# Delta rule on unnormalised queries and keys, with block-diagonal solution and score matrices in its scan

## The reference

```python
def l2_normalize(x):
    return x * lax.rsqrt(jnp.sum(x * x, axis=-1, keepdims=True) + EPS)

def gdn_direction(q, k, v, beta, g):          # 4 heads of 128, chunks of c = 64 tokens
    gc = cumsum(g per chunk)
    decay = exp(gc_i - gc_j) for i >= j, else 0
    kb = k * beta
    lower = strictly lower part of (kb @ k.T) * decay
    u, w = solve(lower + eye, [v * beta, kb * exp(gc)])
    def step(state, ...):
        v_new = u - w @ state
        scores = (q @ k.T) * decay
        out = (q * exp(gc)) @ state + scores @ v_new
        state = state * exp(g_last) + (k * exp(g_last - gc)).T @ v_new
    ...
q, k, v = split(silu(centred_depthwise_conv(q | k | v)))
q = l2_normalize(q) * HD ** -0.5 ; k = l2_normalize(k)
o = forward direction + backward direction
o = o * rsqrt(mean(o * o) + EPS) * norm_g ; y = o * silu(z)
```

## Time and profile before

| | us |
|---|---|
| median of 3 runs | 1723.66 (1723.11 to 1725.65) |
| the profiled execution | 1726.8 |
| its span, first to last instruction | 1725.0 |
| busy: PE, DVE, ACT, POOL | 1687.7, 1160.1, 950.6, 10.1 |

### The profile page before, as it was taken

The page is one execution under the profiler, slowest core; times in us unless marked ns, Lnnn a source line. Parts: engine busy times, 40 slices in busy tenths (PEclk is TensorE's granted clock), DMA queues, the critical chain, the costliest instruction groups (busy, mean ns, idle before and its releaser), DMA issues.

```text
span 1725.0 us, 24744 instructions
## 1 busy us (share of the span) xinstructions
PE 1687.7 (98%) x10220; PEld 1390.6 (81%) x10220; DVE 1160.1 (67%) x1833; ACT 950.6 (55%) x1475; POOL 10.1 (1%) x22
## 2 busy tenths in 40 slices
PE   8999999999999999999999999999999999999998
PEld 6777888877778887888888888888888888878886
DVE  6876886679688667555686467655575556885554
ACT  6743643577155446444566657544464456974443
POOL 0000000000000000000000000000000000000000
PEclk8999999999999999999999999999999999999999
DMA  6322445442234555555644234645555555445543
GB/s 237 123 100 85 178 147 199 171 174 108 77 141 147 191 189 185 193 182 184 220 175 155 100 121 173 234 176 191 218 184 194 186 200 210 148 165 190 191 177 145
DMA packets 41728, 291.77 MB, mean 169 GB/s; under 512 B 4656, under 2 KB 4912, under 8 KB 7440
## 3 DMA queue, kind: packets, MB, share of 16 engines
q1 hardware_dynamic: 39168, 280.23, 45.0%
q0 software_dynamic: 2304, 8.91, 1.5%
q10 hardware_dynamic: 144, 1.05, 0.2%
HBM read 289.12 MB, written 1.05 MB: 168 GB/s over the span
## 4 chain that ended last, share of the span: by engine, by line
PE 81%; DVE 13%; ACT 4%; issue 2%; DMA 0%; DVEq 0%; SPq 0%; ACTq 0%
PE pg L476 24%; PE pg L478 24%; PE pg L477 23%; DVE wl L1948 3%; PE ps L824 2%; PE ps L643 2%; ACT wh L1314 1%; PE ps L867 1%; PE ps L627 0%; ACT hTh L1642 0%; PE ps L926 0%; PE ps L1211 0%; PE ps L1166 0%; DVE hTl L2528 0%; DMA x<-x_in 0%
## 5 line engine op out<-in xcount | busy, mean ns | idle before, releaser
L476 PE MATMUL pg<-wh,hTh 128*128 128x512 f32 x2096 | 836.7, 399 | 5.5 <-DVE wl L2031 3.6
L478 PE MATMUL pg<-wh,hTl 128*128 128x512 f32 x2096 | 819.6, 391 | 0.0
L477 PE MATMUL pg<-wl,hTh 128*128 128x512 f32 x2096 | 818.9, 391 | 0.0
L1948 DVE TENSOR_TENSOR wl<-raw,wh 128x1024 fp32r<-128x1024 f32 x518 | 609.6, 1220 | 191.5 <-ACT wh L1314 188.6
L1314 ACT ACTIVATE wh<-raw 128x1024 fp32r<-128x1024 f32 x528 | 528.8, 1054 | 202.9 <-DMA raw<-weights 192.4
L476 PEld LDWEIGHTS pg<-wh,hTh 128*128 128x128 f32 x2096 | 394.8, 188 | 90.2 <-issue 8.3
L478 PEld LDWEIGHTS pg<-wh,hTl 128*128 128x128 f32 x2096 | 394.7, 188 | 84.5
L477 PEld LDWEIGHTS pg<-wl,hTh 128*128 128x128 f32 x2096 | 395.2, 189 | 75.5
L1414 ACT ACTIVATE arena<-pg,sm 128x256 f32<-128x256 f32 (+1 forms) x67 | 36.6, 546 | 237.7 <-PE pg L478 237.6
L2615 DVE SCALAR_TENSOR_TENSOR arena<-pg,sm,arena 128x256 f32<-128x256 f32 x88 | 38.5, 479 | 155.0 <-ACT arena L1415 155.0
L1369 ACT ACTIVATE hTh<-ps 128x512 fp32r<-128x512 f32 x60 | 33.6, 597 | 31.5 <-PE ps L643 31.5
(11 more groups left out here) (383 smaller groups left out, 1140.1 us busy)
## 6 DMA issues: line engine op xcount, KB each, us to landing
raw<-weights SPq DMA_DIRECT2D x265, 1024.0 KB, 4.8
arena<-wide POOLq DMA_DIRECT2D x9, 512.0 KB, 3.6
raw<-weights ACTq DMA_DIRECT2D x1, 1024.0 KB, 5.5
x<-x_in SPq DMA_DIRECT2D x2, 512.0 KB, 7.5
cst<-const_tables POOLq DMA_DIRECT2D x1, 1024.0 KB, 5.3
plainh<-dist_tables POOLq DMA_DIRECT2D x2, 512.0 KB, 5.7
arena<-gate_mix POOLq DMA_DIRECT2D x1, 1024.0 KB, 7.9
arena<-token_mix POOLq DMA_DIRECT2D x2, 256.0 KB, 5.0
```

The costliest lines, as they stand in the source:

```text
L476: pe.matmul(dst, lh, rh, start=first, stop=False)
L477: pe.matmul(dst, lh, rl, start=False, stop=False)
L478: return pe.matmul(dst, ll, rh, start=False, stop=last)
L1948: tt(wl[:, slot, h], raw[:, slot, h], wh[:, slot, h], ALU.subtract)\
```

## The change

Queries and keys are not normalised any more. The SiLU results of the convolution, which have channels on the partitions, are themselves `qnT` and `knT`; the turns of `features` and their copies fall away, and ScalarE copies the turned-back k into `kn`. VectorE computes all 16 norms at once (`norms`), and they are put where vectors of the right shape are: beta times the key norm (`BETA_NK`) multiplies the values `VS`, half of them on VectorE, half on GpSimd; beta times its square (`BETA_NK2`) takes the place of beta in the lower matrix and goes into `NEGS`; the query norms go into the output's own normalisation. `TB` isn't multiplied by beta any more.

In the scan each head's two 64x64 matrices stand on the diagonal of one 128x128 matrix (`T_DIAG`, `SC_DIAG`), whose other half GpSimd fills with zeros. The scores and the last additions of the inverse are written there by more and smaller instructions; ScalarE copies a part of the inverse. The core of the diff:

```diff
-                gemm(..., inside={(0, 1): second_turn, (1, 0): first_features, (1, 1): cumulated,
-                                                       (1, 3): back_and_rows})
+                gemm(..., inside={(0, 1): second_turn, (1, 1): cumulated, (1, 3): back_and_rows})
...
-                prepare(3)
-                c.wait("qk_ready")
-                features(kn, 2)
-                prepare(3)
-                c.wait("feat_read")
+                prepare(6)
+                c.wait("sq_ready")
+                c.wait("kn_ready")
                 turn_back(2)
...
+                c.wait("vs_ready")
+                c.wait("inv_copied")
+                c.wait("zeros_ready")
...
                     for h in range(NH):
-                        for d, m, r in places[t]:
-                            rhs = RV[half(r), ...] if t else VS[half(r), 0, ...]
-                            last = pe.matmul(ps[half(r), 0, ...], TB4[half(r), 4 * d + h, m, :], rhs, ...)
+                        rhs = RV[:, h * P:(h + 1) * P] if t else VS[:, 0, h * P:(h + 1) * P]
+                        last = pe.matmul(ps[:, 0, h * P:(h + 1) * P], t_diag[:, h, :], rhs, ...)
...
# ScalarE
-                features(qnT, 0)
                 convolved(1)
                 square(1)
+                for m in range(M):
+                    last = act.activation(kn[:, 512 * m:512 * m + 512], ps[:, 2 + m, :], ACT.Copy)
+                last.then_inc(sem["kn_ready"], 1)
...
+                c.wait("inv_yt", 5)
+                for m in range(M):
+                    for r in range(2):
+                        dst, _ = diagonal(2 * m + r)
+                        last = act.activation(dst[half(r), 2:4, half(r)], new[half(r), m], ACT.Copy)
+                last.then_inc(sem["inv_copied"], 1)
# VectorE
-                normalized(0, qn)
...
-                normalized(1, kn)
+                norms()
...
-                    last = dve.tensor_copy(VS[half(r), t, :], ps[half(r), 2 + m, :])
+                    last = tt(heads(VS[half(r), t, :]), heads(ps[half(r), 2 + m, :]), over(BETA_NK[half(r), o:o + 4], P), ALU.mult)
...
-                for d, js in enumerate(both):
-                    last = tt(SC3[:, js, :], SC3[:, js, :], ps[:, 1, :]..., ALU.mult)
+                for r in range(2):
+                    tt(SC6[half(r), :, r, :, half(r)], SC5[half(r), 0], QK4[half(r)], ALU.mult)
+                    for m in range(M):
+                        last = tt(SC6[half(r), 1 - m, 1 - r, :, half(r)], SC5[half(r), 1, m], QK4[half(r), m], ALU.mult)
...
-                c.step(ts(NEGS, EGS, -1.0, None, ALU.mult))
+                for t in range(1, 4):
+                    for d in range(2):
+                        last = stt(NEGS[half(r), 4 * t:4 * t + 4], EGS[half(r), 4 * t:4 * t + 4], -1.0,
+                                   BETA_NK2[half(r), o:o + 4], ALU.mult, ALU.mult)
...
+                c.step(tt(STATS, STATS, NQ2, ALU.mult))
                 rstd_of(STATS, HD)
+                c.step(tt(STATS, STATS, NQ, ALU.mult))
# GpSimd
+                pool.wait_ge(sem["rs_ready"], l + 1)
+                for t in range(4):
+                    for v in diagonal(t):
+                        for r in range(2):
+                            last = pool.memset(v[half(r), :, half(1 - r)], 0.0)
+                last.then_inc(sem["zeros_ready"], 1)
+                c.wait("norms_ready")
+                c.wait("back_read")
+                for t, d in ((0, 0), (1, 0), (2, 1), (3, 1)):
+                    v = heads(VS[half(r), t, :])
+                    last = pool.tensor_tensor(v, v, over(BETA_NK[half(r), o:o + 4], P), ALU.mult)
+                last.then_inc(sem["vs_ready"], 1)
```

More of the change, by code:

```diff
@@ L350, in small_parts, with diagonal @@
             return sw[:, 0:KD * 2 * n].rearrange("p (k t n) -> p k t n", k=KD, t=2)
+        def diagonal(t):
+            cols = 512 * (t % 2)
+            return (heads(v) for v in (T_DIAG[t // 2][:, cols:cols + 512], SC_DIAG[:, 512 * t:512 * t + 512]))
         def times(ap, n):
@@ L397, in program @@
         Lm, LT, X_, XT_, TM_ = V(5120), V(6144), V(7168), V(8192), V(9216)
[L398 removed]
+        SC_, LMASK, SC_DIAG = XT_, TM_, xn
         STATE = V(5120)
@@ L872, in gdn @@
                     for h in range(NH):
[L873 to L876 removed]
+                        rhs = RV[:, h * P:(h + 1) * P] if t else VS[:, 0, h * P:(h + 1) * P]
+                        last = pe.matmul(ps[:, 0, h * P:(h + 1) * P], t_diag[:, h, :], rhs, start=True, stop=True)
                     last.then_inc(sem["uw_done"], 1)
@@ L891, in gdn @@
                     for h in range(NH):
-                        for d, m, r in places[t]:
-                            last = pe.matmul(ps[half(r), 1, h * P:(h + 1) * P], SC4[half(r), 4 * d + h, m, :],
-                                             VN[half(r), h * P:(h + 1) * P], start=True, stop=True)
+                        last = pe.matmul(ps[:, 1, h * P:(h + 1) * P], sc_diag[:, h, :], VN[:, h * P:(h + 1) * P],
+                                         start=True, stop=True)
                     last.then_inc(sem["sv_done"], 1)
@@ L2168, in gdn @@
                     m, r = scan_chunk(t, d)
-                    last = dve.tensor_copy(VS[half(r), t, :], ps[half(r), 2 + m, :])
+                    o = 8 * m + 4 * d
+                    last = tt(heads(VS[half(r), t, :]), heads(ps[half(r), 2 + m, :]), over(BETA_NK[half(r), o:o + 4], P),
+                              ALU.mult)
                 last.then_inc(sem["v_read"], 1)
@@ L2234, in gdn @@
                         c.wait("inv_y")
-                        n = ps[:, 2:4, 256:512].rearrange("p g (q f) -> p g q f", f=CHUNK)
-                        tt(X5[:, :, 1], X5[:, :, 1], n, ALU.add)
-                        c.wait("inv_yt")
[L2238 to L2247, removed]
+                        old, new = (v.rearrange("p g (h m f) -> p m g h f", m=M, f=CHUNK)
+                                    for v in (X_.rearrange("p (g n) -> p g n", g=2)[:, :, 256:512], ps[:, 2:4, 256:512]))
+                        for m in range(M):
+                            for r in range(2):
+                                dst, _ = diagonal(3 - 2 * m - r)
+                                tt(dst[half(r), :, half(r)].rearrange("p (g h) f -> p g h f", g=2), old[half(r), m],
+                                   new[half(r), m], ALU.add)
+                        c.wait("inv_yt")
+                        old, new = (v.rearrange("p (h m f) -> p m h f", m=M, f=CHUNK)
+                                    for v in (XT_[:, 0:256], ps[:, 0, 0:256]))
+                        for m in range(M):
+                            for r in range(2):
+                                dst, _ = diagonal(2 * m + r)
+                                last = tt(dst[half(r), 0:2, half(r)], old[half(r), m], new[half(r), m], ALU.add)
+                        c.sig(last, "inv_scaled")
                 prepare(1)
```

73 lines of the change are left out of this document (36 added, 37 removed).

## The result

| kernel | median | runs | lowest to highest | profiled execution | its span |
|---|---|---|---|---|---|
| before | 1723.74 us | 6 | 1722.92 to 1725.65 | 1726.80 | 1725.0 |
| after | 1730.50 us | 6 | 1727.96 to 1732.28 | 1729.91 | 1728.1 |

The ratio is 1.0028 with a 95% interval of 1.0019 to 1.0038: slower by 3.3 to 6.6 us. The prediction said 1729.5.

The account below looks back on a forecast made before the run. VectorE was taken to bound the kernel up to the inverse, TensorE behind it. GpSimd's contention of +6.0 us and -0.2 for the rest gave +5.8, so 1729.5 us from a 1723.7 median; 80% range 1720.5 to 1734.5.

Parts of the forecast that it names:

- case (a): Whole kernel: GpSimd's multiplies hold up VectorE, +6.0 us, the rest -0.2; 1729.5 us, chance 0.47.
- Rival (b): Whole kernel: GpSimd's work is free and the other effects cancel; 1723.5 us, chance 0.33.
- Part 7: GpSimd's multiplies before the inverse hold up three VectorE instructions: 3.0 us a layer lost, 6 in all.
- Part 1: q's norm and turns go, before k's taps on VectorE: 1.85 us a layer gained of 5.2 removed.
- Part 2: k's norm becomes `norms` on VectorE: 0.7 us lost, 0.37 gained at v's turn; `low_ready` 1.55 us sooner so far.
- Part 3: Scores written into block diagonals on VectorE, between `low_ready` and the inverse: 2.7 us for 1.29, 1.4 a layer lost.
- Part 4: End of the inverse on VectorE: additions 2.4 us against 2.6, 0.1 gained; `NEGS` as six instructions, 0.4 lost.
- Part 5: Scan's products on full matrices: bursts still 1.00 us, entering cheaper by 0.13 each; five count, 0.65 a layer gained.
- rival (c): Scan's full-matrix bursts cost by instructions, under 0.7 us each: about 5.5 us faster in all, 1718.2, chance 0.15.
- Part 6: Output's norm: two more small dependent instructions before `y_ready`, 0.4 us a layer lost.
- parts 1 to 6: All effects but GpSimd's contention, from q's norm to the output's: 0.1 us a layer gained, 0.2 in all.
- Rival (d): TensorE's longer waits drop its clock to 1.2 GHz as the inverse starts: 1.7 us a layer more, 1733, chance 0.05.

Follow-up runs that it names:

- e1: The kernel after with GpSimd's four multiplies of the values left out (output not the reference's): 1725.66 us, 1.0004 of before.
- e2: The kernel after with the four multiplies made by ScalarE late in the inverse instead of by GpSimd: 1724.96 us, 0.9999 of before.
- e8: The kernel after with GpSimd's four multiplies held back until the second level of the inverse: 1725.03 us, 0.9995 of before.
- e3: The kernel before with the same four GpSimd multiplies added at the same place, by ones: 1733.22 us, 1.0041 of before.
- e5: e2 without the block diagonals and zero fills; scan, scores and end of the inverse as before: 1719.71 us, 0.9964 of before.
- e4: The kernel after without GpSimd's multiplies, its sixteen write-only zero fills moved to their place: 1725.94 us, 1.0005 of before.
- e6: e5 with VectorE's retention masks and `NEGS` moved into the levels of the inverse: 1715.38 us, 0.9946 of before.
- e7: The kernel before with only the retention masks moved into the levels of the inverse: 1721.27 us, 0.9981 of before.

## Why the prediction was right, and where its terms were not

The forecast was case (a), GpSimd in VectorE's way, with all else cancelling. The first half is shown by experiments: with the multiplies gone, done elsewhere, or done later, the change is at 1.0004, 0.9999 and 0.9995 of before (e1, e2, e8); with the multiplies alone, the kernel before loses 4.8 to 9.1 us (e3). Rival (b), GpSimd free, falls with e3 and e8. The second half, the cancelling, came out in the sum, with help from a term that the prediction didn't have.

The profiled executions can be divided at four instructions of each layer: from the start of the convolution of q to the end of `low_ready`, on to the first step's copy of the new values (L2267), on to the last step's copy, and on to TensorE's product at `y_ready` (L643). Each cell has the first and the second layer, in us:

| kernel | to `low_ready` | to the first copy | to the last copy | to L643 |
|---|---|---|---|---|
| before | 52.46, 52.64 | 48.69, 48.48 | 33.42, 33.44 | 25.27, 25.03 |
| after | 53.69, 53.86 | 49.59, 51.72 | 32.26, 32.26 | 25.43, 25.43 |
| e8 | 51.14, 51.31 | 49.57, 51.34 | 32.24, 32.25 | 25.43, 25.43 |
| e3 | 55.77, 55.94 | 49.34, 49.32 | 33.43, 33.41 | 25.26, 25.04 |
| e5 | 51.16, 51.32 | 46.38, 46.34 | 33.41, 33.41 | 25.42, 25.42 |

After takes 1.1 us more than before in the first layer and 3.7 in the second, 4.8 together, which is what the ratio says; the rest of that pair of executions differs by 1.7 the other way. The first column shows the contention alone: 2.55 us a layer between e8 and after, 3.3 between before and e3. By parts:

- **Part 7, contention.** Taken at 3.0 us a layer as three VectorE instructions held up, the second L1948 and both L2178. It was these three, each held up by 0.83 to 0.85 us and not by 1.0: 2.5 us. GpSimd's instruction was allowed 1.38; alone it takes 1.05, beside VectorE 1.7. The Trainium skill (SBUF — State Buffer, Who interferes with whom) says that a VectorE instruction with two SBUF inputs contends with a GpSimd instruction that reads SBUF and not with one that only writes. The runs agree: the pair L2175 takes 2.98 beside the multiplies and 1.29 beside the fills of e4, and L2178, with an input in PSUM, 1.23 beside the multiplies. The estimate of 3.4 us a layer by the page's figure for GpSimd came from nearly the right duration (1.1 estimated, 1.05 measured), but VectorE lost 2.5 us, less than the whole of three of them.
- **Part 1.** 1.85 us a layer predicted. In the second layer the convolution of q starts 0.87 later than before (VectorE's first taps at 363.77 against 362.90), and k's sum 0.92 sooner (388.91 against 389.83): 1.8 gained.
- **Part 2.** `norms` takes 5.81 us (from 388.91 to 394.72) against 5.01 before. The predicted loss of 0.7 had the 0.2 of beta's copy already taken off; on the same terms 0.6 were lost. The 0.37 for L709's lateness brought 0.1: VectorE's own L1944 ends at 400.72 and L2166 follows at once, so VectorE hadn't been waiting for TensorE there. `low_ready` comes 1.2 later, counted from the same start (2.10 - 0.87); less the contention's 2.5 that is 1.3 sooner, not 1.55. The new wait at the turn of v was taken at 1.7 and is 1.65.
- **Part 3.** The scores take 2.7 us, as worked out, by four rows of VectorE from 421.27 to 424.0, of which these are the first two:

```profile
421.27 0.68 DVE L2197 TENSOR_TENSOR xn<-arena,ps 64x512 f32<-64x512 f32 x1
421.88 0.73 DVE L2199 TENSOR_TENSOR xn<-arena,ps 64x256 f32<-64x256 f32 x2
```

- **Part 4** was mis-sized. The eight last additions take 2.9 us and not 2.4 (a pair of 64x256 0.85, a pair of 64x128 0.6), so 0.3 is lost where 0.1 was to be gained; TensorE waits 0.7 for them (L870). `NEGS` costs 3.25 - 2.48 = 0.77 from the start of L1944 to that of L2275, where I had 0.4: each of the six costs 0.14.
- **Part 5** was mis-sized the other way. A burst of the scan on full matrices, by TensorE's timeline of after, against the earlier trace rows:

```profile
471.84 0.39 PE L486 MATMUL pg<-wh,hTl 128*128 128x512 f32 x1
472.07 1.05 PE L886 MATMUL ps<-arena,xn 128*128 128x128 f32 x8
472.88 0.48 PE L484 MATMUL pg<-wh,hTh 128*128 128x512 f32 x1
```

  It holds TensorE for 472.88 - 472.07 = 0.81 us, not 1.00, and its entry takes 0.23 as predicted. So a burst saves 0.3 us and not 0.13. My row for it, L941 of the retention stage, had 0.2 more; it was followed by another burst on full matrices, and whether that is the reason isn't shown. This is a part of rival (c), which wanted under 0.7. The gain did arrive: from the first copy to the last the scan is 1.2 us a layer shorter, in every kernel with block diagonals, where 0.65 was predicted.
- **Part 6.** 0.4 us were to be lost at `y_ready`. From the scan's last copy to L643's product the kernel after takes 0.2 and 0.4 us more. TensorE's wait there grew from 0.2 in all to 1.9, by more than that, since TensorE is there earlier.
- **A stop of TensorE that the prediction left out.** The prediction called TensorE nearly always busy in the inverse, with short waits. The view behind the earlier trace rows also has a stop of 1.2 us there that nothing in the trace explains, and the first layer one of 1.4 (the last section). After has one of 1.6, in the second layer only. That is 1.0 us gained which no part foresaw, and luck for the forecast. By an estimate from the terms above, parts 1 to 6 lose 0.3 us a layer, 0.6 in all, and with it 0.4 are gained; the table has e8 0.7 below before.
- **Rival (d), the clock.** It did fall, in both layers (0.83 in 84 to 92, 0.57 in 416 to 424). e8 has the same instructions on VectorE and TensorE, and its clock is at 1.00 behind `low_ready`:

```profile
416.00:424.00 8.00, 6.22 (x87) 4.95 (x86) 7.82 (x13) 7.85 (x9) 0.00 (x0) 1.00 0.37 133
```

  From `low_ready` to the first copy it is as fast as after in the first layer and 0.4 us faster in the second (e1, without the multiplies: 49.66 and 51.40). So the clock cost after at most about 0.4 us, by one trace of each; the prediction's 1.7 a layer isn't seen.

The cancelling of parts 1 to 6 is what e5 takes apart. Without the block diagonals the kernel is 5.4 us faster than before by the medians, 6.5 by the table: 2.6 won before `low_ready`, 4.5 between it and the first copy, and 0.5 lost at the end. But of the 4.5, 2.6 are the stops of TensorE, which e5 doesn't have, and why it hasn't isn't known. So the removal of the norms by itself is worth about 4 us by the table, an estimate. The block diagonals cost VectorE 3.2 us a layer (1.4 at the scores, 1.8 at the end of the inverse) and give 1.2 back in the scan: about 4 us of the 5 to 6 between e2 and e5, and a stop of 1.4 is the rest.

## What to carry to other kernels

GpSimd seems free here and isn't, when it reads SBUF beside VectorE instructions that read two inputs from SBUF: before GpSimd is given work, look for such instructions in that stretch, and if the result isn't needed for a long time, hold GpSimd back with a wait. Making TensorE's instructions fewer and larger pays only if the engine that feeds it has slack: count the writes that the new layout wants on that engine (eight small ones of 2.9 us for two of 1.1, and 1.4 us more at the scores) against what the bursts save (0.3 us each, 1.2 in a scan). And where one engine works almost without a gap for 18 us ahead of a hand-over, moving its unurgent work past it (e6, e7) pays until the next wait shows: of 4.4 us moved, 2.0 were won, and then VectorE waited for ScalarE.

## What the runs showed that I hadn't expected

- Apart from each other, GpSimd's four multiplies take 4.22 us and VectorE's four instructions 3.65, 7.87 together. Side by side they run from 403.48 to 410.48, 7.0 us: nearly in turns, and both lose 2.5 to 2.6.
- A VectorE copy of 128x16 within one buffer took 1.01 us beside them, six times its 0.17 (e3). It lost 0.84 us, as the instructions of 128x512 and of 128x1024 did: in these traces the price of one hold-up doesn't depend on the size of what is held up. A TENSOR_SCALAR of 128x512 lost 0.3 in four beside fills that read nothing (e4).
- TensorE stops for 1.2 to 1.6 us in the middle of some bursts of the inverse, at the same line and with nothing in the trace that it waits for: "issue" in the waits. The kernels built on the one before have it in both layers (before, e3, e7), those built on the one after in the second layer only (after, e1, e2, e4, e8), and e5 and e6 not at all. Here is one in the kernel before, within a burst of 128 on TensorE's timeline:

```profile
448.65 2.89 PE L824 MATMUL ps<-arena 64*64 64x64 f32 x123
452.72 0.38 PE L824 MATMUL ps<-arena 64*64 64x64 f32 x5 [1.18 <-issue]
```

  It takes 1.0 us off the difference between before and after. The two profiled executions also stand 3.1 above and 0.6 below their kernels' medians. What causes the stops stays open.
